# Queries at latent tokens alone, retention steps pipelined by one, modulation columns by transposes, in a three-layer block chain

## What is computed

```python
def modulate(t, gain, shift, scale):
    return rmsnorm(t, gain) * (1 + scale) + shift
# mod = silu(c) @ w_mod + b_mod and mod_c = silu(c_ctx) @ w_mod + b_mod, six column sets each, per layer

# first block: the delta net, of which only the latent tokens' output is used
qkv = jax.nn.silu(conv_fn(p_qkv, conv_w))
q, k, v = split_cols(qkv, (DN_KEY, DN_KEY, DN_VAL))
q = l2norm(q) * (DN_DK ** -0.5)
k = l2norm(k)
oc, s_ctx = gated_delta_chunked(context, s0)      # its state is used, its output oc is not
ol, _     = gated_delta_chunked(latent, s_ctx)

# second model, layer 0: retention, both directions, chunks of 128 tokens
scores = jnp.einsum('bhnid,bhnjd->bhnij', qc, kc) * decay
intra = jnp.einsum('bhnij,bhnje->bhnie', scores, vc)
kv_local = jnp.einsum('bhnjd,hj,bhnje->nbhde', kc, k_dec, vc)
s, s_prev = lax.scan(lambda s, kv: (chunk_decay * s + kv, s), s0, kv_local)
inter = jnp.einsum('bhnid,hi,nbhde->bhnie', qc, q_dec, s_prev)
```

## Time and profile before

| | us |
|---|---|
| median of 3 | 1926.28 |
| lowest, highest | 1925.98, 1929.57 |
| the profiled execution | 1927.05 |
| its span, first to last instruction | 1925.3 |
| TensorE busy | 1802.2 (94%) |
| VectorE busy | 849.4 (44%) |
| ScalarE busy | 757.4 (39%) |
| GpSimd busy | 484.9 (25%) |

### The profile page before, as it was taken

How to read it: one execution, slowest core, us unless ns; L and a number is a source line. 1 busy time by engine, 2 the same in 40 slices (tenths; PEclk the granted TensorE clock), 3 DMA queues, 4 the chain that set the end, 5 groups by cost and what they waited for, 6 DMA issues and landing times.

```text
span 1925.3 us, 34986 instructions
## 1 busy us (share of the span) xinstructions
PE 1802.2 (94%) x14968; PEld 1561.9 (81%) x14968; DVE 849.4 (44%) x1643; ACT 757.4 (39%) x1330; POOL 484.9 (25%) x256
## 2 busy tenths in 40 slices
PE   5998998888799999998999899999999989999998
PEld 3787997778689999787788677888888767689998
DVE  1647226566244333534477734221221346744343
ACT  3453532233335555522345334222222343755443
POOL 0136222121113443111134111121112211124443
PEclk7999999999899999899999899999999999999999
DMA  8443244232264554423211123323322336144553
GB/s 319 176 157 139 90 174 154 90 111 89 78 255 176 182 190 154 155 86 107 79 68 67 67 90 133 149 88 131 128 91 104 115 135 228 66 154 170 181 178 129
DMA packets 36584, 261.63 MB, mean 136 GB/s; under 512 B 4048, under 2 KB 4176, under 8 KB 6224
## 3 DMA queue, kind: packets, MB, share of 16 engines
q1 hardware_dynamic: 36432, 259.40, 37.4%
HBM read 258.34 MB, written 1.05 MB: 135 GB/s over the span
## 4 chain that ended last, share of the span: by engine, by line
PE 83%; DVE 8%; ACT 4%; issue 3%; DMA 2%; POOL 1%; SPq 0%; DVEq 0%; ACTq 0%
PE ps L876 20%; PE ps L878 19%; PE ps L877 19%; PE ps L927 3%; PE ps L903 2%; PE ps L893 1%; PE ps L1180 1%; PE ps L895 1%; PE ps L894 1%; PE ps L935 1%; PE ps L1168 1%; PE ps L1186 1%; PE ps L986 1%; PE ps L1019 1%; PE ps L1020 1%
## 5 line engine op out<-in xcount | busy, mean ns | idle before, releaser
L767 POOL TENSOR_TENSOR wl<-raw,wh 128x1024 fp32r<-128x1024 f32 (+1 forms) x179 | 426.6, 2384 | 1155.1 <-ACT wh L1583 1155.1
L876 PE MATMUL ps<-h_hi,wh 128*128 128x256 f32 (+1 forms) x1696 | 552.5, 326 | 4.9 <-POOL wl L767 4.2
L877 PE MATMUL ps<-h_lo,wh 128*128 128x256 f32 (+1 forms) x1696 | 547.5, 323 | 0.0
L878 PE MATMUL ps<-h_hi,wl 128*128 128x256 f32 (+1 forms) x1696 | 547.5, 323 | 0.0
L1583 ACT ACTIVATE wh<-raw 128x1024 fp32r<-128x1024 f32 (+1 forms) x330 | 342.2, 1040 | 401.1 <-PE ps L878 292.7
L876 PEld LDWEIGHTS ps<-h_hi,wh 128*128 128x128 f32 x1696 | 326.2, 192 | 31.7 <-POOL wl L767 5.3
L878 PEld LDWEIGHTS ps<-h_hi,wl 128*128 128x128 f32 x1696 | 326.0, 192 | 23.8
L877 PEld LDWEIGHTS ps<-h_lo,wh 128*128 128x128 f32 x1696 | 326.3, 192 | 23.3
L2100 DVE TENSOR_TENSOR wl<-raw,wh 128x1024 fp32r<-128x1024 f32 (+1 forms) x151 | 189.0, 1252 | 266.5 <-ACT wh L1583 266.2
L876 PE MATMUL ps<-gh,wh 128*128 128x256 f32 (+1 forms) x528 | 169.2, 320 | 0.0
L877 PE MATMUL ps<-gl,wh 128*128 128x256 f32 (+1 forms) x528 | 168.1, 318 | 0.0
(11 more groups left out here) (423 smaller groups left out, 2655.0 us busy)
## 6 DMA issues: line engine op xcount, KB each, us to landing
raw<-in_mod SPq DMA_DIRECT2D x72, 1024.0 KB, 4.9
raw<-in_ffn_in SPq DMA_DIRECT2D x66, 1024.0 KB, 4.8
raw<-in_ffn_out SPq DMA_DIRECT2D x24, 1024.0 KB, 4.8
raw<-in_w_in SPq DMA_DIRECT2D x16, 1024.0 KB, 4.8
raw<-in_w_gate SPq DMA_DIRECT2D x12, 1024.0 KB, 4.8
raw<-in_w_ab SPq DMA_DIRECT2D x12, 1024.0 KB, 4.9
raw<-in_ffn_out SPq DMA_DIRECT2D x12, 768.0 KB, 4.2
raw<-in_w_at SPq DMA_DIRECT2D x5, 1024.0 KB, 4.9
```

The lines of the kernel that those rows point to most:

```text
L767: nc.gpsimd.tensor_tensor(wl[e % SPLIT][:, 0:entries[e]["words"]], part(e), wh[e % SPLIT][:, 0:entries[e]["words"]].bitcast(F32), ALU.subt ...
L876: nc.tensor.matmul(b[:, cols], wh[e % SPLIT][:, w], xh(k), start=(k == 0), stop=False)
L877: nc.tensor.matmul(b[:, cols], wh[e % SPLIT][:, w], xl(k), start=False, stop=False)
L878: ins = nc.tensor.matmul(b[:, cols], wl[e % SPLIT][:, w], xh(k), start=False, stop=(k == nk - 1))
```

## The change

Three independent parts, and the code that goes with them.

1. The columns of `w_in` and of the convolution weights are ordered keys, queries, values on the host. Queries are tiles 4 to 7 and projected, convolved, squared and normed at latent tokens alone. Keys are tiles 0 to 3.
2. The retention loop scores for step s+1 at the start of step s, and VectorE masks them one step ahead, into two buffers in turn (`PTr2`). Decayed keys and queries are made by GpSimd, the queries one step ahead, into two buffers (`qd2`).
3. Modulation rows are turned by two transposes, and VectorE sums the four partials (reduction) and adds the bias in a second instruction with both operands in SBUF.

```diff
+        pool.wait_ge(sem("r_state"), 1)
+        evacuated(pool, "rkt", NC - 1)
+        for s in range(NC):
+            if s < 3:
+                if s > 0:
+                    full(pool, "RU", s - 1)
+                for d, c in enumerate(chunk_of(s)):
+                    kdec = tin2[:, 8 * d:8 * d + 8].unsqueeze(2).to_broadcast([P, 8, 64])
+                    nc.gpsimd.tensor_tensor(kd2[:, d].rearrange("p t (i e) -> p (t i) e", i=2),
+                                            lkt[:, c].rearrange("p t (i e) -> p (t i) e", i=2), kdec,
+                                            ALU.mult).then_inc(sem("r_kd"), 1)
+                if s > 1:
+                    full(pool, "RO", s - 1)
+                for d, c in enumerate(chunk_of(s + 1)):
+                    nc.gpsimd.tensor_tensor(qd2[(s + 1) % 2][:, d], lq[:, :, CH * c:CH * c + CH], QD[:, d],
+                                            ALU.mult).then_inc(sem("r_qd"), 1)
...
                 for i in range(2):
-                    ins = nc.tensor.matmul(b[:, 2 * i:2 * i + 2], modrow[:, (n - 1) % 2, P * i:P * i + P], S("pick"),
-                                           start=True, stop=True)
+                    ins = nc.tensor.transpose(b[:, P * i:P * i + P], modrow[:, (n - 1) % 2, P * i:P * i + P], ident)
...
+        def latent_spread(key, src):
+
+            b, rn = begin(*key), slice(64, P)
+            for g in (2, 3):
+                ins = nc.tensor.matmul(b[:, P * g:P * g + P], ident[rn, 32 * g:32 * g + 1].to_broadcast([64, P]),
+                                       src[rn, :], start=True, stop=True)
+            close(ins)
...
         for m in range(2, 12):
-            hdense(("qkv", m), ALL)
+            hdense(("qkv", m), LAT if 4 <= m < 8 else ALL)
...
-                        group_sums(("l2", m), CA("ones")[:, 0:32], sqr[:, m % 2, :])
+                        group_sums(("l2", m), CA("ones")[:, 0:32], sqr[:, m % 2, :], range(4) if m < 4 else (2, 3))
...
+        scores("RS", 0, 0)
         for s in range(NC):
             cf, cbk = chunk_of(s)
-            scores("RS", s, cf)
+            if s < 3:
+                scores("RS", s + 1, s + 1)
...
-                    free(V.tensor_tensor(mods[:, lay, 2 * c:2 * c + 2, :],
-                                         bank("modcol", n)[:, 0:4].rearrange("p (m v) -> p m v", m=2), bias,
+                    parts = bank("modcol", n)[:, 0:256].rearrange("p (m j r) -> p m r j", m=2, j=4)[:, :, 0:2, :]
+                    link(V.tensor_reduce(mods[:, lay, 2 * c:2 * c + 2, :], parts, AX.X, ALU.add))
+                    free(V.tensor_tensor(mods[:, lay, 2 * c:2 * c + 2, :], mods[:, lay, 2 * c:2 * c + 2, :], bias,
                                          ALU.add), "modcol", n)
...
-            conv(cy[:, m % 2, :], cb[:, m % 3, :], S("dconv")[:, 3 * m:3 * m + 3], 516).then_inc(sem("conv_sum"), 1)
+            at, n = (L + 1, 259) if 4 <= m < 8 else (0, 516)
+            conv(cy[:, m % 2, at:], cb[:, m % 3, at:], S("dconv")[:, 3 * m:3 * m + 3], n).then_inc(sem("conv_sum"), 1)
...
+        retained(0)
         for s in range(NC):
             cc = chunk_of(s)
...
             if s < 3:
+                retained(s + 1)
```

More of the change, by code:

```diff
@@ L1110, in _ @@
                 pe.wait_ge(sem("conv_done"), 12)
-            for what, src in (("ktok", qk[:, 4:8, :]), ("vtok", vT[:])):
+            for what, src in (("ktok", qk[:, 0:4, :]), ("vtok", vT[:])):
                 b = begin(what, c)
@@ L1698, in _ @@
                 full(act, "qkv", m)
-                A(cb[:, m % 3, 1:1 + L], bank("qkv", m)[:, 0:L], ACT.Copy)
+                only = 4 <= m < 8
+                if not only:
+                    A(cb[:, m % 3, 1:1 + L], bank("qkv", m)[:, 0:L], ACT.Copy)
+                lat = bank("qkv", m)[:, 0:L] if only else bank("qkv", m)[:, L:T]
                 free(A(cb[:, m % 3, L + 2:L + 2 + 4 * (GRID + 1)].rearrange("p (r w) -> p r w", r=4)[:, :, 0:GRID],
-                       bank("qkv", m)[:, L:T].rearrange("p (r w) -> p r w", r=4), ACT.Copy), "qkv", m)
+                       lat.rearrange("p (r w) -> p r w", r=4), ACT.Copy), "qkv", m)
             if m >= 1:
@@ L1705, in _ @@
                 act.wait_ge(sem("conv_sum"), i + 1)
[L1706 removed]
+                if not 4 <= i < 8:
+                    A(dst[:, 0:L], cy[:, i % 2, 0:L], ACT.Silu)
                 A(dst[:, L:T].rearrange("p (r w) -> p r w", r=4),
```

77 lines of the change are left out of this document (36 added, 41 removed).

## The result

The changed kernel takes 1899.26 us (median of four, 1898.91 to 1903.7) beside 1927.92 us for the kernel before in the same comparison. The ratio is 0.9858, with a 95% interval of 0.9836 to 0.9879, so some 27 us are gone (23 to 32). I had forecast 1906.0 us, 20.3 us less, in a range of 1898 to 1915. The sign, the order of size and the range held. The gain was 7 to 8 us larger than the sum, and the experiments show that this was no sum of small errors: one term was mis-sized by 7 to 13 us. That the result still lies inside the range, 1.3 us above its lower end, is in part luck: I had drawn that end for another reason (modulation steps that turn out free), and the gain that brought the result there was in no term.

The account below looks back on a forecast made before the run. TensorE, with 83% of the chain that ended last, was taken as the bound. The terms -10.4 + 0.3 - 2.4 - 5.7 - 4.5 + 2.4 = -20.3 us gave 1906.0 us from a median of 1926.28, range 1898 to 1915.

Parts of the forecast that it names:

- modulation steps that turn out free: Lower end of the modulation term: steps charged 0 gain too, some 6 us more; forecast's own lower end 1899.
- Queries at latent tokens only: qkv tiles 4 to 7 at 256 columns: two pairs lose 5.2 us each, -10.4 us, with 0.3 charged for late weights.
- Rival 1: Narrow qkv pairs wait 2 us more each for weights, the tile after too; 5 us come back: 1911; chance 0.10.
- L2 norms: Norms of the four query tiles: sums (0.36 us) and spreads (0.92 us) halve, together -2.4 us.
- Retention loop: Scores and masks one step ahead remove TensorE's two waits per step; steps of 6.65 us, sum -5.7 us.
- Rival 2: Retention step stays at about 8 us because GpSimd or VectorE's order comes last: 1909; chance 0.07.
- Modulation columns: Two transposes replace four TensorE instructions, 0.25 us saved in 18 of 72 steps: -4.5 us; delta net +2.4 us.
- 0 for all of these: No gain for modulation steps at waits: the first eight, those before a norm's spread, six among attention projections.
- Held additions: Delta net: bias additions reading SBUF twice are held by GpSimd products, 0.6 us net for each chunk, +2.4 us.
- Rival 3: Each of 16 delta net additions waits out a GpSimd product, attention ones a subtraction: +10 us, 1916; chance 0.08.
- Rival 4: Transposes before dense stretches lower the clock to 1.2 GHz: 27 us added, 1933 us; chance 0.03.
- Rival 5: Shorter qkv only lengthens the wait at the end of the chain behind ba; 10 us stay: 1916; chance 0.04.

Follow-up runs that it names:

- no_q: The changed kernel without queries at latent tokens: w_in in the old column order, all at 512 columns, norms included; 1907.20 us, ratio 0.9893.
- wide_pick: The kernel before with the two small modulation-column products widened to use 128 columns of constants instead of two; 1918.03 us, ratio 0.9937.
- only_m: The kernel before with the new modulation columns alone (two transposes, a reduction, an addition); 1913.63 us, ratio 0.9916.
- no_r: The changed kernel with the retention loop as before; 1906.53 us, ratio 0.9895, with a fourth execution of 3440.19 us left out.
- psum_sum: The changed kernel with VectorE's sum of the four modulation partials kept in PSUM, where the bias addition reads it; 1900.98 us, ratio 0.9842.

## Why the prediction was right, and where its sum was wrong

**Queries at latent tokens only: right.** Charged with their steps -11.6 us for the stage, measured -11.7. The weights were the risk, and the two narrow pairs show no wait. Rival 1 falls.

**L2 norms: the term was twice too large.** I halved the times with the number of instructions. PE timeline of after, one group of them:

```profile
184.80 0.41 PE L993 MATMUL ps<-sqr,const_all 128*32 128x128 f32 x4
185.14 0.71 PE L1001 MATMUL ps<-l2c,const_all 64*128 64x128 f32 x4
185.78 0.39 PE L895 MATMUL ps<-h_hi,wh 128*128 128x256 f32 x1
```

Half the sums take 0.34 us where all took 0.36, and half the spreads 0.64 where all took 0.92. Four groups save some 1.2 us, not 2.4. And behind the wait for `l2c` of 2.15 us, which both kernels have, the clock is now 0.54 for 3.7 us (window above), which gives back 1.6 us: 18 products where 31 stand in the same time in `before`. The stage comes out at +1.2 us, of which 0.8 us is then still unaccounted for. The stretch is not the work of the narrow norms, as `no_q` shows.

**Retention loop: right**, to 0.1 us in the trace and by its own reasons: steps of 6.61 us, GpSimd's four products 4.5 us, the one wait where I had put it. Rival 2 falls. (The first step keeps a wait for its masked scores, 0.48 us now, as I had said it would.)

**Modulation columns: the mechanism that I described is right and small, the one that I left out is large.** The step is 0.20 us where I had said 0.21, and the 7 steps in the FFNs gave 1.9 us for 1.75. But the part as a whole is worth 10.0 us (undone) to 14.9 us (alone), where -4.5 and the +2.4 of the delta net made -2.1 (another -0.75 stood in the loop's term). The failing step is "0 for all of these", said of the steps that wait anyway. At those places the length of the step is indeed worth nothing. What counts is that TensorE, in a stretch with waits, now moves 128 columns where it moved 2, and is granted 2.4 GHz for more of the time. `wide_pick` isolates this at 10.5 us with no instruction shortened.

**Held additions: the right mechanism, priced a third too high, and without effect.** Nine of the 16 additions in the delta net take 0.51 to 0.59 us, the others 0.16. TensorE's waits for `mods` ahead of L954 (L935 before) rose from 0.7 us (three, in the kernel before) to 3.1 us (four):

```profile
301.29 1.07 PE L946 MATMUL ps<-raw,small 128*32 128x256 f32 x16
303.14 0.41 PE L954 MATMUL ps<-const_all,modrow 128*128 128x128 f32 x2 [0.78 <-DVE mods L2153]
303.48 1.15 PE L1194 MATMUL ps<-d_TTc,d_Xc 64*64 64x64 f32 x32
```

From the start of the last modulation step of a chunk to the level products it is now 2.19 us (301.29 to 303.48) in all four chunks, where it was 1.80 us in three and 1.54 us in one: 1.8 us more in all, with the shorter column step in it, against 2.4 charged. With the sum in PSUM it is 1.85 us. The stage as a whole is 0.1 us shorter all the same. Its granted clock rose from 0.96 to 0.99, which is the likely reason; the shorter column steps are not, for the waits inside a chunk take them back (305.19 to 314.15 us before, 292.32 to 301.29 now, from the first to the fourth step of the first chunk). Taking the holds away changes nothing in the time that these runs can tell. Rival 3 falls.

**Rival 4, the transposes lower the clock: falls as a whole.** The granted clock of every kernel with transposes is above that of every kernel with the narrow products. The row that should have warned me stood in my own argument: the old instruction is 128x2. I wrote that "matmuls with 128 columns of real data give way to transposes", and it was two columns that gave way to 128. The rule that I cited then, from the Trainium skill ("TensorE: Matmul & The Clock Gate", section "Part 4: PE-mode transpose"), says that transposes don't count as a busy TensorE. By it I had 27 us on top of my sum, 1933 us, and measured 1899.26. Whether transposes count for less than ordinary products of the same width stays open: `only_m`, with two instructions of 128 columns, has 0.974 to 0.979, and `wide_pick`, with four, 0.979 to 0.982, and the first 60 us sort the same way (0.83 to 0.89 against 0.91 and 0.94), but the two differ in number as well. One local loss goes with the transposes: the stretch at 1.2 GHz behind the wait for `l2c` stands in both profiles of the changed kernel, in `no_r`, `no_q` and `psum_sum` (0.54 to 0.56 for 3.7 us), and in none of the six kernels with four products, where the clock there is 1.00. It costs some 1.6 us. `only_m` has transposes and does not have it, and no modulation step stands within 60 us ahead of that wait, so that they are its cause is not shown.

**Rival 5 falls**: nothing of the `qkv` gain was given back in the chain behind `ba`, which takes 32.0 us both times (125.62 to 157.57 us before, 111.54 to 143.50 us now).

What stays open: why a wait is followed by 1.2 GHz in one kernel and not in another (the wait for `l2c` is 2.15 us in both), the stalls of about 3 us without a releaser in single executions, the one execution of `no_r` at 3440.19 us, and a few us between the sum of the parts alone (14.9 + 4.2 + 11.9 = 31 us), the parts undone (10.0 + 7.6 + 2.4 to 9.2 = 20 to 27 us) and the change itself (23 to 32 us).

## What to carry to other kernels

Where TensorE is the bound, read the granted clock beside the instruction times. 1 minus it, times the span, is an upper bound of what the clock can give back: 0.033 of 1925 us, 64 us. It is not an estimate, for TensorE also stands waiting at 1.2 GHz; here `wide_pick` gained 10.5 us and the wide fillers 12 to 14. An instruction that is free because it stands in a wait can still decide at which clock the work behind the wait runs. In this kernel wide work in a wait was worth having, even work of no use (75 idle products, the fastest version of this study at 1885.90 us), and narrow work in its place was not (1901.73 us). It pays only where nothing else takes over: at the first of the six waits the clock doubled and the time stayed. And halving the instructions of a short step need not halve its time. Here eight to four took the sums from 0.36 to 0.34 us and the spreads from 0.92 to 0.64 us, while four products to two transposes took the columns from 0.46 to 0.20 us: measure what one of them adds.

## What the runs showed of the hardware

- Products of no use (256 or 512 columns) before the end of a wait came with a granted clock of 1.00 behind all six waits, where it was 0.50 to 0.60 without them. With products of two columns in their place, over about the same time, it was 0.50 to 0.61 again behind five of the six, and 1.00 behind one.
- A wait of 2.15 us was followed by a granted clock of 0.54 for 3.7 us in the changed kernel and by 1.00 in the kernel before.
- Four products with 128 columns take as long as four with 2 columns here, 0.47 us against 0.46 us, so the width was free.
- The executions of one kernel differ in time largely as their clocks do: of 41 of the kernel before the fastest took 1922.37 us at 0.971 and the slowest 1944.96 us at 0.955.
- A VectorE addition of 128x4 with both operands in SBUF, 0.16 us otherwise, took 2.2 us beside a GpSimd subtraction of 2.4 us (578.02 us in the first profile of the changed kernel). With its operand in PSUM the longest of 72 was 0.164 us.
